# The opening of a one-core block kernel: modulation in pairs of shift and scale, with norm and first projection between them

## What is computed

```python
silu_c, silu_cc = jax.nn.silu(c), jax.nn.silu(c_ctx)
mod_l = (silu_c @ mod_w[0] + mod_b[0]).reshape(bsz, 6, 1, D)      # 6 parts: shift, scale, ...
mod_c = (silu_cc @ mod_w[0] + mod_b[0]).reshape(6, 1, D)
h_lat = rms_norm(lat, g) * (1 + mod_l[:, 1]) + mod_l[:, 0]        # 512 tokens
h_ctx = rms_norm(cx, g) * (1 + mod_c[1]) + mod_c[0]               # 256 context tokens
# gla_mixer: z = h @ w_in gives q, k, v, r and 32 low-rank columns glr
# g = log_sigmoid(glr @ w_gate + b_gate) / 16, then a scan over chunks, both directions
```

## Time and profile before

| | us |
|---|---|
| median of 3 runs | 1680.24 (1679.89 to 1681.18) |
| profiled execution | 1685.94 |
| its span, first to last instruction | 1684.2 |
| TensorE busy | 1624.8 |
| DVE busy | 834.6 |
| ACT busy | 486.6 |
| GpSimd busy | 113.4 |

### The profile page before, as it was taken

One profiled execution on the slowest core, in us unless ns is written; L12 is line 12 of the kernel. 1 busy time (PEld: TensorE's weight loads), 2 busy tenths in 40 slices (PEclk: granted clock), 3 DMA queues, 4 the chain that ended last, 5 costly groups with the idle time before them and its releaser, 6 DMA issues.

```text
span 1684.2 us, 19430 instructions
## 1 busy us (share of the span) xinstructions
PE 1624.8 (96%) x7870; PEld 1358.3 (81%) x7870; DVE 834.6 (50%) x1006; ACT 486.6 (29%) x550; POOL 113.4 (7%) x96
## 2 busy tenths in 40 slices
PE   8898999989999999989999999999999999999997
PEld 3688999878888888877888888878877888888885
DVE  3878655464333333564444443345455544444443
ACT  3444246432222223332222222231222322222220
POOL 0000000020000000030000001216004000000000
PEclk9899999979999999989999999999999999999998
DMA  8343530122222223322222223242212222222231
GB/s 361 142 150 103 197 123 29 68 83 75 100 93 85 96 78 97 101 100 75 100 100 99 85 78 94 93 163 83 93 50 76 75 100 100 100 100 62 95 104 65
DMA packets 32981, 171.33 MB, mean 102 GB/s; under 512 B 3104, under 2 KB 3360, under 8 KB 19104
## 3 DMA queue, kind: packets, MB, share of 16 engines
q1 hardware_dynamic: 32928, 170.58, 29.0%
HBM read 168.47 MB, written 2.10 MB: 101 GB/s over the span
## 4 chain that ended last, share of the span: by engine, by line
PE 72%; issue 22%; DVE 4%; ACT 1%; DMA 1%; POOL 0%; SPq 0%; POOLq 0%; DVEq 0%; ACTq 0%
PE bank L494 71%; DMA mod_raw<-in_mod 1%; DVE mod_sum L1453 1%; ACT w_hi L1055 1%; DVE tmp L1488 1%; DVE w_lo L1432 0%; DMA mod_w<-in_mod 0%; DVE y_ffn L2107 0%; DVE a_lo L1820 0%; DVE a_lo L1481 0%; PE bank L702 0%; PE bank L758 0%; POOL root L402 0%; DVE hc_lo L1481 0%; DVE glr L1543 0%
## 5 line engine op out<-in xcount | busy, mean ns | idle before, releaser
L1432 DVE TENSOR_TENSOR w_lo<-w_raw,w_hi 128x2048 fp32r<-128x2048 f32 x142 | 329.2, 2318 | 389.3 <-ACT w_hi L1055 389.0
L494 PE MATMUL bank<-a_hi,w_hi 128*128 128x512 f32 x1248 | 493.8, 396 | 16.1 <-DVE a_lo L1820 9.2
L494 PE MATMUL bank<-a_lo,w_hi 128*128 128x512 f32 x1248 | 490.9, 393 | 0.0
L494 PE MATMUL bank<-a_hi,w_lo 128*128 128x512 f32 x1248 | 490.3, 393 | 0.0
L1055 ACT ACTIVATE w_hi<-w_raw 128x2048 fp32r<-128x2048 f32 x144 | 275.5, 1914 | 600.2 <-PE bank L494 598.7
L494 PEld LDWEIGHTS bank<-a_hi,w_hi 128*128 128x128 f32 x1248 | 237.5, 190 | 68.9 <-issue 18.2
L494 PEld LDWEIGHTS bank<-a_lo,w_hi 128*128 128x128 f32 x1248 | 237.6, 190 | 50.0 <-issue 0.7
L494 PEld LDWEIGHTS bank<-a_hi,w_lo 128*128 128x128 f32 x1248 | 237.4, 190 | 49.9
L494 PE MATMUL bank<-g_hi,w_hi 128*128 128x512 f32 x528 | 205.4, 389 | 0.0
L494 PE MATMUL bank<-g_lo,w_hi 128*128 128x512 f32 x528 | 205.4, 389 | 0.0
L494 PE MATMUL bank<-g_hi,w_lo 128*128 128x512 f32 x528 | 205.4, 389 | 0.0
(11 more groups left out here) (276 smaller groups left out, 1576.0 us busy)
## 6 DMA issues: line engine op xcount, KB each, us to landing
w_raw<-in_ffn_in SPq DMA_DIRECT2D x66, 1024.0 KB, 4.8
w_raw<-in_ffn_out SPq DMA_DIRECT2D x24, 768.0 KB, 4.2
mod_raw<-in_mod SPq DMA_DIRECT2D x16, 1024.0 KB, 5.2
w_raw<-in_ffn_out SPq DMA_DIRECT2D x24, 640.0 KB, 3.9
w_raw<-in_gla_in SPq DMA_DIRECT2D x12, 1024.0 KB, 4.8
w_raw<-in_mix_in SPq DMA_DIRECT2D x10, 1024.0 KB, 4.7
mod_w<-in_mod SPq DMA_DIRECT2D x8, 1024.0 KB, 15.7
xT<-in_x_fm SPq DMA_DIRECT2D x2, 2048.0 KB, 12.5
```

Of the source, the lines that this page charges most:

```text
L494: return pe.matmul(out, lhs, rhs, start=first, stop=last, skip_group_check=True)
L1432: V.tensor_tensor(flat(w_lo[s]), flat(w_raw[s]), flat(w_hi[s]).bitcast(F32), ALU.subtract).then_inc(lo_done[s], 1)
```

## The change

The modulation is made in four pairs, each of a shift unit p and a scale unit 4 + p, which serve the chunks 2p and 2p + 1. The stationary operand is widened with zeros to 32 columns (`sc_wide`), the rows have 32 partitions, and the turning operand is a sum of four blocks of the identity (`turn`). x is loaded in four quarters. After each pair DVE makes columns, gains and the norm of two chunks, and TensorE puts those chunks of the first key unit between the pairs. The second key unit follows next, mixed with the end of the first; the context's squares, sums, roots and norm come after the fourth pair of x. The roots are spread with four matmuls each (`first_roots`) instead of DVE's diagonal. The low-rank products use banks 6 and 2, both context key products follow them, the queries keep banks 0 and 1. On DVE two modulation parts stand between the two splits of the query weights in place of three ahead of the first, and one more part falls into the first turn of the loop over heads.

```diff
+            load_mods(0)
+            for i in range(4):
+                sp.dma_start(xT[:, 2 * i:2 * i + 2], a["x_fm"][:, 2 * i:2 * i + 2]).then_inc(x_loaded[i], 16)
             sp.dma_start(flat(w_raw[0]), a["gla_in"][0]).then_inc(raw_loaded[0], 16)
+            for p in range(1, 4):
+                load_mods(p)
+            sp.dma_start(flat(w_raw[1]), a["gla_in"][1]).then_inc(raw_loaded[1], 16)
+            sp.dma_start(cT[:], a["ctx_fm"]).then_inc(c_loaded, 16)
             sp.dma_start(small_raw[:], a["rank_w"]).then_inc(rank_loaded, 16)
-            sp.dma_start(flat(w_raw[1]), a["gla_in"][1]).then_inc(raw_loaded[1], 16)
...
-            load_parts(2, 7)
+            load_parts(2, 6)
             for m in range(4, 8):
                 load(m % 2, a["gla_in"][m])
-            for m, q0, q1 in ((8, 7, 9), (9, 9, 11), (10, 11, 13), (11, 13, 16)):
+            for m, q0, q1 in ((8, 6, 9), (9, 9, 11), (10, 11, 13), (11, 13, 16)):
```

TensorE:

```diff
+            def mod_lines(p):
+                b = (2, 4)[p % 2]
+                if p >= 2:
+                    pe.wait_ge(rows_copied, p - 1)
+                for w, n in enumerate((p, 4 + p)):
+                    pe.wait_ge(mod_w_loaded[n], 16)
+                    for k in range(KD):
+                        m = mm(bank[b][0:32, w * UC:(w + 1) * UC], sc_wide[:, k], mod_w[n][:, k], k == 0, k == KD - 1)
+                m.then_inc(rows_ready, 1)
...
+            mod_lines(0)
+            pe.wait_ge(streamed_sum, KD)
+            token_sums(6, 0, sq_sum, T, True, True).then_inc(sums_ready, 1)
+            first_roots(6, PAIRS, 1)
+            pe.wait_ge(turn_set, 3)
+            mod_columns(0)
+            mod_lines(1)
+            pe.wait_ge(lo_done[0], cnt.next(lo_done[0]))
+            for p in range(1, 4):
+                k_part(0, (2 * p - 2, 2 * p - 1))
+                mod_columns(p)
+                if p < 3:
+                    mod_lines(p + 1)
+            pe.wait_ge(lo_done[1], cnt.next(lo_done[1]))
+            k_part(1, range(4))
+            k_part(0, (6, 7))
+            pe.wait_ge(streamed_sum, 2 * KD)
+            token_sums(5, 0, dec_k[1], TC, True, True).then_inc(sums_ready, 1)
+            k_part(1, (4, 5))
+            first_roots(5, TC // P, 2)
+            k_part(1, (6, 7))
...
+            low_rank()
+            context_keys_of(0, 5)
+            filled[5] = True
+            context_keys_of(1, 2)
             mod_map(0)
-            gla_unit(1, (3, 4), 5)
-            mod_map(1)
             pe.wait_ge(rank_lo, 3)
...
             gates(0)
             gates(1)
-            gla_unit(2, (0, 1), None)
+            unit(0, (0, 1), (a_hi, a_lo))
+            mod_map(1)
             gates(2)
             gates(3)
-            gla_unit(3, (0, 1), None)
+            unit(1, (0, 1), (a_hi, a_lo))
```

ACT and DVE:

```diff
+            stream_squares(xT, T, range(4))
             copy_rows(0)
+            stream_squares(xT, T, range(4, KD))
+            split_hi(0)
+            first_his(0)
             copy_rows(1)
+            first_his(1)
+            copy_rows(2)
+            first_his(2)
+            split_hi(1)
+            copy_rows(3)
+            first_his(3)
             act.wait_ge(c_loaded, 16)
+            stream_squares(cT, TC, range(KD), 2)
...
+            stream_sums(sq_sum, T)
             mean_square(6, PAIRS, D)
+            split_lo(0)
...
+            for p in range(4):
+                if p == 3:
+                    split_lo(1)
+                pair_mods(p)
+                first_norm(p)
+            dve.wait_ge(norm_lo, cnt.now(norm_lo))
+            stream_sums(dec_k[1], TC, 2)
             mean_square(5, 2, D)
...
             norm_parts(cT, 5, lambda m: gain[:, 1, m:m + 1], TC, hc_hi, hc_lo, lambda m: mod[:, m, 1:2])
-            split_lo(1)
             mod_parts(0, 2)
...
-            mod_parts(2, 5)
+            dve.wait_ge(ready[5], cnt.next(ready[5]))
+            V.tensor_copy(kcT[:, 0:2].rearrange("p a b -> p (a b)"), bank[5][:]).then_inc(free[5], 1)
+            split_lo(0)
+            mod_parts(2, 4)
             dve.wait_ge(ready[2], cnt.next(ready[2]))
...
             split_lo(1)
...
-            parts_at = (5, 7, 10, 13, 16)
+            parts_at = (4, 7, 10, 13, 16)
```

More of the change, by code:

```diff
@@ L220, in build @@
         x_var = place("x_var", [P, PAIRS])
+        turn = place("turn", [P, 2])
         cols = place("cols", [P, NCOLS])
@@ new lines, in mod_columns, with first_roots @@
+            def mod_columns(p):
+                pe.wait_ge(rows_copied, p + 1)
+                if p:
+                    pe.wait_ge(cols_added, p)
+                for w in range(2):
+                    for c in range(CPU):
+                        j = w * KD + CPU * p + c
+                        m = mm(bank[7][:, 2 * j:2 * j + 2], mod_rows[p % 2][0:32, w * UC + c * P:w * UC + (c + 1) * P], turn[0:32],
+                               True, True)
+                m.then_inc(cols_ready, 1)
+            def first_roots(b, n, count):
+                pe.wait_ge(root_done, count)
+                for t in range(n):
+                    m = mm(bank[b][:, t * P:(t + 1) * P], root4[:, t:t + 1].to_broadcast([P, P]), ident[:], True, True)
+                m.then_inc(roots_ready, 1)
@@ new lines, in k_part @@
+            def k_part(u, ks):
+                for k in ks:
+                    pe.wait_ge(norm_lo, cnt.upto(norm_lo, k + 1))
+                    for c in range(CPU):
+                        b = 3 * u + c
+                        m = mm3(bank[b][:], weights(u, k, c), (a_hi[:, k], a_lo[:, k]), k == 0, k == KD - 1)
+                        if k == KD - 1:
+                            m.then_inc(ready[b], 1)
+                            filled[b] = True
+            mod_lines(0)
+            pe.wait_ge(streamed_sum, KD)
@@ L1149, in _ @@
             copy_out(1, kT[:, 1])
-            act.wait_ge(ready[2], cnt.next(ready[2]))
-            split_hi(0)
             copy_out(3, kT[:, 2])
@@ L1154, in _ @@
             act.wait_ge(ready[5], cnt.next(ready[5]))
+            split_hi(0)
+            act.wait_ge(ready[2], cnt.next(ready[2]))
             split_hi(1)
@@ new lines, in _, with pair_mods @@
+            dve.wait_ge(roots_ready, cnt.next(roots_ready))
+            dve.wait_ge(cols_loaded, 16)
+            def pair_mods(p):
+                j = slice(CPU * p, CPU * (p + 1))
+                dve.wait_ge(cols_ready, p + 1)
+                V.tensor_tensor(mod[:, 0:2 * KD].rearrange("p (w j) v -> p w j v", w=2)[:, :, j],
+                                bank[7][:, 0:4 * KD].rearrange("p (w j v) -> p w j v", w=2, v=2)[:, :, j],
+                                spread(col("mod_b", 0, 2 * KD).rearrange("p (w j) -> p w j", w=2)[:, :, j], 3, [P, 2, CPU, 2]),
+                                ALU.add).then_inc(cols_added, 1)
+                dve.wait_ge(cols_added, p + 1)
+                for u in range(2):
+                    V.scalar_tensor_tensor(gain[:, u, j], mod[:, KD + CPU * p:KD + CPU * (p + 1), u], 1.0,
+                                           col("norm_g", CPU * p, CPU), ALU.add, ALU.mult).then_inc(mods_done, 1)
+                    cnt.expect(mods_done)
+                dve.wait_ge(mods_done, cnt.now(mods_done))
@@ new lines, in first_norm @@
+            def first_norm(p):
+                for m in (CPU * p, CPU * p + 1):
+                    if m >= 2:
+                        dve.wait_ge(norm_lo, cnt.now(norm_lo, 1 - m % 2))
+                    V.scalar_tensor_tensor(tmp[m % 2][:], xT[:, m], gain[:, 0, m:m + 1], bank[6][:], ALU.mult, ALU.mult).then_inc(scaled, 1)
+                    cnt.expect(scaled)
+                for m in (CPU * p, CPU * p + 1):
+                    dve.wait_ge(norm_hi, cnt.next(norm_hi))
+                    V.scalar_tensor_tensor(a_lo[:, m], tmp[m % 2][:], mod[:, m, 0:1], a_hi[:, m].bitcast(F32),
+                                           ALU.add, ALU.subtract).then_inc(norm_lo, 1)
+                    cnt.expect(norm_lo)
```

155 lines of the change are left out of this document (55 added, 100 removed).

## The result

The change made the kernel a little slower. The changed kernel takes 1687.98 us (median of 5, 1685.23 to 1689.55), the kernel before 1679.99 us (median of 5, 1679.52 to 1681.18): a ratio of 1.0043 with a 95% interval of 1.0030 to 1.0056. In a second comparison, again unchanged (a_same), it came to 1689.65 us against 1682.53, a ratio of 1.0041 (1.0026 to 1.0056). Predicted were 1677.4 us and a range up to 1681.5. So the prediction was wrong, in sign and in size. The kernel before is less steady than the 0.1% of its first three runs: 30 later runs lie between 1679.83 and 1685.84 us, which is 0.36%.

A forecast was written before the change was run, and what follows sets the result against it. TensorE, busy 96% of 1684.2 us, was taken as the bound, with 14 us of opening waits and low clock to win. Gates come 4.3 us earlier, 2.8 us reach the end: median 1680.24 becomes 1677.4, range 1672.5 to 1681.5.

The forecast's parts named there:

- Step 1 and 2: Opening: modulation pair 0 ends at 17.25 us; then TensorE idles 4.3 us for the squares' sums and its clock falls.
- Loads and the wide stationary operand: Opening: nothing waits for loads; 32 stationary columns instead of 2 cost nothing, 3.1 us at most if they showed.
- Bank 2: Before the second context keys: DVE frees the bank at 91.0 us, TensorE needs it at 91.65, 0.65 us of slack.
- The rival in which it came late: Second context keys: bank 2 freed late, TensorE waits and its clock falls; 1684.2 us at 4 us lateness; chance 0.11.
- Step 3: Opening at 1.2 GHz: token sums to 23.5 us, GpSimd's root 1.01 us, spread roots to 27.1, columns 0 to 28.85.
- Step 4: Modulation pair 1: low clock until about 33.7 us costs 2.4 us; pair ends at 38.15, or 35.7 to 39.5.
- Step 5: From pair 1's end to the gates: TensorE fed without gaps, 53.5 us to 91.65; gates at 98.2, 4.3 us earlier.
- the rival "the gain is used up": Head 0 and context key: DVE's waits 2 us above count, or wider weight loads show; 1679.2 to 1681.5 us; chance 0.20.
- Part 6, "these land at about 109 and 135, wanted at 110 and 142": Head 0: parts 4 and 5 land at about 109 us, part 6, issued after weights 7, at 135, before DVE wants them.
- After that both orders are alike.: Behind head 0: the orders match, so the 2.8 us gain stays to the end, 1684.2 becoming 1681.4 us in profile.
- I take the difference as the same for both kernels.: Whole kernel: the profiled execution's 5.7 us above the median holds for both kernels, so 1680.24 us becomes 1677.4.

The follow-up runs named there:

- a_squares: The changed kernel with ACT's copy of pair 0's rows moved behind all eight squares of x; 1684.52 us, ratio 1.0010 to the kernel before.
- a_last: a_early_root with modulation units between TensorE's small matmuls, a sixth part summed ahead of the gates, context token sums and roots one chunk pair later; 1673.21 us, ratio 0.9934.
- a_early: a_squares with parts 0 to 2 in memory of their own, loaded early, summed in DVE's opening idle, and mod_map(0) ahead of the low-rank product; 1679.85 us, ratio 0.9983.
- a_root: The changed kernel with DVE waiting for GpSimd's inverse root before it splits the first unit's weights; 1687.86 us, ratio 1.0028 to the kernel before.
- b_parts: The kernel before with only the modulation parts rescheduled: one fewer ahead of the gates, one more in head 0, SP's loads following; 1686.30 us, ratio 1.0019.
- a_early_root: a_early with DVE waiting for the inverse root before its first split; 1680.68 us, ratio 0.9987 to the kernel before.

## Why the prediction was wrong

Right, by its own steps:
- *Step 1 and 2.* Pair 0 was done at 16.36 (17.25 predicted), the new idle time was 4.31 us (4.3), the clock fell in it, and the copy ahead of squares 4 to 7 was the cause of 2.0 us of it: 2.28 us are left in a_squares.
- *Loads and the wide stationary operand.* In the view of tile mod_w the load has a median of 0.110 us, where before had 0.085:

```profile
L501 PEld LDWEIGHTS bank<-mod_w,sc_wide x128: 106/110/178, 7.1 to 60.9; 128*32 128x32 f32 x128
```

  That is 25 ns more for 30 columns, and it cost nothing: 32 records at the full clock take 7.09 us in a_last, 7.07 before. As an increment this is what the Trainium skill (TensorE: Matmul & The Clock Gate, section LDWEIGHTS (loading the stationary operand)) gives for 30 columns; the price it would have had unhidden doesn't show.
- *Bank 2.* TensorE didn't wait for it: DVE had done the low-rank subtraction and stood idle for 0.78 us when the first context keys were ready (0.65 us of slack predicted):

```profile
91.29 2.29 DVE L1620 TENSOR_TENSOR glr<-bank,glr 32x512 fp32r<-32x512 f32 x4
94.35 0.69 DVE L1623 COPY kcT<-bank 128x512 f32<-128x512 f32 x1 [0.78 <-PE bank L501]
```

  The rival in which it came late was not what happened, although it was the one with the right sign.

Wrong:
- *Step 3, the root at 1.01 us.* It took 2.92, as DVE's split, which the new order puts right behind the mean square, began 0.23 us before it and runs beside it. The earlier trace rows was measured with no split beside it (before begins the split at 37.28, after the root), and I carried its price over without asking what DVE does meanwhile. Term missed: 1.9 us. The Trainium skill (SBUF — State Buffer, section SBUF: two separate sides) states an exclusive lock of the port pair that VectorE and GpSimd share, held for a whole instruction; the trace agrees, as the root ends 0.87 us after the split does, both here and in a_early, a_root removes it, and in a_squares the root, begun first, isn't held up. It doesn't show the other side of such a lock: the split of a_squares begins 0.08 us behind the root and takes 2.29 us, no longer than elsewhere.
- *Step 4, the length of the low clock.* I counted the small matmuls from 21.5 on as the restart and let it end at 33.7. It ended at 35.5 in this execution and 34.2 in a_same. Together with the root this is why pair 1 ended at 39.54 instead of 38.15, the outer end that the step itself named (39.5).
- *Step 5.* From there to the gates I counted 60.05 us and TensorE took 61.19, all of it work: 1.1 us. Of this 1.0 lies between 39.54 and 65.37, where two modulation pairs, three chunk pairs and three groups of columns took 25.83 us and my prices give 24.8. In all, the gates came 2.5 us later than predicted, the first context key 2.25 us later. Of the 2.8 us of gain 0.5 was left at this point. That is the size of the rival "the gain is used up", but not its mechanism: it counted on DVE's waits, and TensorE's own root, low clock and work took the gain.
- *Part 6, "these land at about 109 and 135, wanted at 110 and 142".* This step failed outright. Its load waits for part 4's buffer, and part 4 is the very part that the change moved into head 0, so it is issued at 141.97, not behind weights 7, and lands at 147.1. DVE waits 2.03 us for it and copies head 0's bank 2 at 149.94, where I had 146. I followed SP's queue by the weights ahead of it and not by the wait of its own. b_parts shows it without the new opening.
- *"After that both orders are alike."* They are in code, not in time. With less slack on DVE the waits of before come back larger: 2.80 for 2.34 in head 1, 2.51 for 1.06 at the last modulation sum. Together with head 0's 1.1 us and 0.3 more at 129.16 (1.21 for 0.95) the waits behind the first context key are 3.2 us longer, and 10.2 us of low clock stand there for 6.8, another 1.7. That turns the -0.5 us of the first context key into the +4.5 us of the FFN's first matmul, to within 0.1 us.
- *"I take the difference as the same for both kernels."* The profiled execution of the kernel before took 5.7 us more than the median, at a mean clock of 0.978; that of the changed kernel took the median itself, 1687.98. So the difference of the two profiles, +1.8 us, is not that of the kernels, and a forecast carried from a profile to a median has this error on top.

The medians differ by 7 to 8 us, more than the 4.5 of the profiles. Each run comes with its mean granted clock (to 0.001, which is 1.7 us), and the clock accounts for most of the difference: over 6 runs a_same has 0.9762, over 17 the kernel before has 0.9799. With half speed as the only other level, these are 80 and 68 us at the low clock, 12.8 us more, worth up to 6.4 us (less by half of what TensorE is idle in them, 3.3 of the 13.7 us of a_same's opening). Time multiplied by mean clock, averaged, is 1649.1 for a_same and 1648.7 for the kernel before. By this measure the low clock makes up nearly all of the 7.1 us between these two medians; 3.5 to 7 us of the added low clock lie in the first 225 us (the table). It doesn't mean that the waits won and lost cancel: in the profiles they are 3.2 us longer in a_same (19.8 against 16.6). The product counts a wait at the low clock by half only, which takes up a part of that; the rest isn't accounted for. The same product is 1643.0 for a_last, so that one also has less waiting. Why the rest of the low-clock time differs, in code that is the same, stays open; the kernel before alone varies from 0.978 (1685.3 us) to 0.982 (1679.5 us) between runs.

## What to carry to other kernels

Follow a moved transfer by the wait that it has of its own (here its buffer) and not by its place in the queue, above all when the change moves the work that frees the buffer. Before an operation's price is carried to a new place, look at what runs beside it there: a small GpSimd operation on a critical handover should not meet a long VectorE operation that began before it. And when waits are removed from an engine whose helper is nearly full, count the helper's slack at every later wait, and give the engine a large piece of work to do at each handover, so that neither the wait nor the low clock appears.

## What the runs showed of the hardware

- A root of 128x4 elements on GpSimd takes 1.01 us alone (a_root, a_early_root) and 2.92 to 3.14 us when a VectorE operation of 128x2048 with two operands from memory began 0.23 or 0.02 us before it (after, a_early); it then ends 0.87 us behind that operation in both. When the VectorE operation began 0.08 us after it, it took 1.01 us (a_squares).
- The time from TensorE's last wait to the full clock differed: 5.8 and 7.4 us in the kernel before, 6.7 us in a_squares (20.45 to 27.10), 9.6 us in the changed kernel (25.87 to 35.50). From 20.68 to 25.87 us of the changed kernel, with 8 small records and a wait of 3.32 us, it was at 0.50 throughout.
- With whole modulation units between the small groups it stayed at 1.00 (a_last, 16 to 90 us).
- In a_last the first loads of the modulation units begin 0.43 us apart from 7.08 to 10.50 us, twice the pitch of 0.216 us later on, while the table of stretches gives 1.00 for 7 to 11 us. So the pitch, and not this column, tells the speed at the start.
- The same 1306 to 1311 us of code differ by up to 4.5 us between executions, and the longer ones have more time at 0.50.
